# Sample attention by pairs of batches: pages gathered once, keys and values in 32-column groups, block choice inside the prompt attention

## The chip, the cores and the metric

One core of a Trainium2 chip runs the whole program. The time is that of the device for one execution, in microseconds; every kernel's time is the median of its runs.

## What is computed

One layer of a decoder trunk for two groups of tokens that share all weights: a prompt of 256 tokens, and a sample group of 8 sequences ("batches") with one new token each and 2048 past tokens in caches. Everything is float32. A layer is: adaLN factors from c, norm, one projection, two attentions, a gated merge, an output projection, norm, a gated feed-forward (FFN, 5632 wide), a down projection, norm.

For the sample group the attention reads its caches:

```python
past_cmp = cache_cmp[layer, page_table]               # 16 pages of 128 rows for each batch
kvc = _compress(concat([past_cmp, kv_cmp]), ...)      # 127 compressed blocks
o_cmp, p_cmp = _cmp_attend(q_nsa, kvc, pos)
idx = _select_blocks(p_cmp, pos, ns)                  # 16 of 33 blocks of 64, for each kv head
g_past = pool_blk[phys, :, :, hidx]                   # cache_sel: k and v of the chosen blocks
o_sel = _sel_attend(q_nsa, kvg, idx, pos)
o_win = attend(q_nsa, concat([cache_win, kv_win]))    # 512 past rows
o_nsa = g[0] * o_cmp + g[1] * o_sel + g[2] * o_win
# dilated: 12 heads of 128, three groups, 128 past keys each at stride 1, 4, 16
p = softmax over each group; o_dil = the groups mixed by their softmax denominators
```

There are 16 query heads of 64 in 2 kv groups; a page row holds k and v of both groups, 256 floats.

## The kernel before, in words

Each engine's stream is written out by hand in one program: `block.sync` (SP issues most loads), `block.gpsimd` (POOL issues the page gathers and the cache copies), `block.tensor`, `block.scalar`, `block.vector`. Engines wait for one another by semaphores: `pe_.mark("used", u)` names a point of TensorE's stream, and `wait_ge(*pe_.at("used", u))` waits for it. Stages run one after another:

1. adaLN parts 0 and 1 with the compression of the sample pages, then the projection in 51 chunks.
2. The prompt attention: 40 units (`UNITS`, first 32 "n" units of the 16 NSA heads by two query blocks, then 8 "d" units of the dilated heads). In iteration u TensorE does `scores(u)`, one step `ada(NA1 + u)` of the other 32 adaLN steps (each 8 products of 32 x 512 columns in four groups of 32 PSUM rows on a 2 MB piece of `w_ada`, through a ring of three slots), `probs(u - 1)` and `pv(u - 2)`. VectorE does the unit's maximum and scaling, ScalarE the exponential and the PSUM copies.
3. The sample attention. The compressed keys come back from DRAM (`kv_kept`), `cs` gives the compressed scores of all 8 batches (128 rows: batch by head), VectorE ranks the blocks and makes the mask `am`. Then, for each batch, five groups of four 128x128 turns of keys (16 tiles of pages, 4 of the window), each copied to `KS` by ScalarE or VectorE in turn and multiplied by a 128-column `qbd` in which only that batch's 16 columns are not zero (L918, L928). One softmax over 128 x 2576, 22 turns, and for each batch 23 products with 16 columns of probabilities (L958 to L962). Pages are gathered twice, once for the keys and once for the values (16 gathers of 2 MB through the three slots), the window's keys and values too (16 loads of 256 KB through two buffers). The dilated part does the same: 24 steps of four turns and four products (L980, L990), a softmax over 32 rows, `PTm` (the probabilities spread with an identity), 96 products (L1011) and 12 for the new token (L1017).
4. Merge, output projection (`wout`), FFN, `down`: float32 products split into three float32r products each (L1033 to L1035), with weights through four slots; ScalarE makes the high part (L1419), VectorE the low part (L1900). The sums of squares for the last two norms are products with a matrix of ones, one for each of 16 tiles (`stat`, L670; `last_stat`, L1113).

POOL also copies the caches to the outputs, paced by the progress of the projection, of the FFN and of `down`.

Of the kernel before, what the change touches and what calls it, by code (L numbers as in the profile page):

```python
# [25 lines left out]
P = 128  # L26
# [33 lines left out]
S0 = "new_nsa"  # L60
_c = 0
for _n, _w in (("ident", P), ("rot_nsa", P), ("rot_dil", P), ("ones", P), ("part8", 8), ("cos_nsa", T), ("sin_nsa", T),
               ("cos_dil", T), ("sin_dil", T), ("causal", 3 * P), ("dilmask", 9 * P),
               ("cmp_add", QT * NBP), ("cmp_mul", QT * NBP), ("rowsel", P), ("head_of", H),
               ("new_nsa", B), ("new_dil", B), ("group", B * KVH), ("spread", P), ("keep", NSEL), ("force", NSEL),
               ("head_cols", HG * RD), ("before", NSEL * NSEL), ("eye", RD * RD)):
    CONST[_n] = (_c, _w)
    _c += _w
# [5 lines left out]
def constants():  # L74
# [34 lines left out]
    own = np.where(np.eye(B, dtype=bool), 0.0, NEG)  # L109
# [4 lines left out]
    put("new_nsa", own[row // H])  # L114
    rd = np.arange(RD)
    put("new_dil", own[rd // HG])
    group = (row // G)[:, None] == np.arange(B * KVH)[None, :]
    put("group", group)
    put("spread", group.T)
# [4 lines left out]
    put("head_cols", np.broadcast_to(rd[None, :] % HG == np.arange(HG)[:, None], (B, HG, RD)))  # L124
    j = np.arange(NSEL)
    put("before", np.broadcast_to(j[None, :] < j[:, None], (H, NSEL, NSEL)))
    put("eye", np.broadcast_to(np.eye(RD), (P, RD, RD)))
# [57 lines left out]
def program(nc, i_, o_, ctx, seen):  # L185
# [32 lines left out]
    def const(name):  # L218
        c, w = CONST[name]
        if c < CONST_P:  # L220
            return c_all[:, c:c + w]
        return {"before": before_c, "eye": eye_c}.get(name) if name in ("before", "eye") \
            else c_sample[:, c - CONST_P:c - CONST_P + w]
# [34 lines left out]
    gatesS = part(3)  # L258
    CMP0 = top[0]
# [24 lines left out]
    sbase = [qk0]  # L284

    def spart(words):
        a = sbase[0]
        sbase[0] += words
        assert sbase[0] <= tmV0 + QT * DHEADS * P, sbase[0] - tmV0 - QT * DHEADS * P
        return mem[:, a:a + words]  # L290
    KS = spart(4096)
    wide = spart(3072)
    SS = wide[:, 0:2576]
    rk = wide[:, 0:NSEL * NSEL].rearrange("p (j i) -> p j i", i=NSEL)
    qpad = wide.rearrange("p (j b r) -> p j b r", j=DHEADS, b=B)
    wide2 = spart(3072)
    before_c = wide2[:, 0:NSEL * NSEL]
    PTn = wide2[:, 0:22 * P].rearrange("p (j r) -> p j r", r=P)
    PTm = wide2.rearrange("p (g r c) -> p g r c", g=NG, r=RD)
    c_sample = spart(CONST["before"][0] - CONST_P)  # L300
    vcS = spart(B * P).rearrange("p (b f) -> p b f", f=P)
    qbd = spart(B * P).rearrange("p (b r) -> p b r", r=P)
    ptc = spart(P)
    pcmp = spart(P)
    kcS = wide2[:, 1096:1096 + B * P].rearrange("p (b n) -> p b n", n=P)
    am = spart(NSEL)
    imp = spart(4 * NSEL)
    sel = spart(4 * NSEL).rearrange("p (j i) -> p j i", i=NSEL)
    eye_c = w1p.rearrange("p s l j e -> p (s l j e)")[:, 0:RD * RD]
    late = mem[:, at0 + 1540:at0 + 2352]  # L310
    qfull, dqnew = late[:, 0:P], late[:, P:P + 96].rearrange("p (j b) -> p j b", b=B)
    dknew = late[:, 224:320].rearrange("p (j b) -> p j b", b=B)
    knew = late[:, 320:336].rearrange("p (j b) -> p j b", b=B)
    Ed = late[:, 336:336 + 408]

    qn = mem[:, at0:at0 + 384].rearrange("p (j r) -> p j r", r=RD)
    Pn = mem[:, at0 + 384:at0 + 768].rearrange("p (g h r) -> p g h r", g=NG, h=HG)
    oR = wide[:, 0:B * P].rearrange("p (b f) -> p b f", f=P)
    win = mem[:, at0:at0 + 1024].rearrange("p (u t f) -> p u t f", u=2, t=4)
    oRd = mem[:, at0 + 768:at0 + 768 + P]  # L320
# [3 lines left out]
    xs8 = rstd[:, 0:B].unsqueeze(1)  # L324
# [76 lines left out]
    loaded = [signal(f"slot{s}_loaded") for s in range(4)]  # L401
# [4 lines left out]
    sample_const = sem("sample_const")  # L406
# [6 lines left out]
    win_in = [signal(f"window{s}_in") for s in range(2)]  # L413
# [9 lines left out]
    nf_sq, nf_used = sem("last_norm_squares"), sem("last_norm_squares_used")  # L423
# [40 lines left out]
    UNITS = [("n", qt, h) for h in range(H) for qt in range(QT)] + [("d", qt, h) for h in range(HG) for qt in range(QT)]  # L464
# [17 lines left out]
    def _(sp):  # L482
# [20 lines left out]
        for c, (col, n) in enumerate(CHUNKS):  # L503
# [4 lines left out]
            sp.dma_start(chunk_piece(chunk_low(c), c, F32), rows(w_in, slice(col, col + n))).then_inc(*proj_in[c % 4].mark("proj", c, by=16))  # L508
        for a in range(NA1, NA1 + 3):
# [5 lines left out]
        sp.wait_ge(*dve_.at("sample_q"))  # L515
        before_at, eye_at = CONST["before"][0], CONST["eye"][0]
        sp.dma_start(c_sample, i_["const"][:, CONST_P:before_at]).then_inc(sample_const, 16)
        sp.dma_start(before_c, i_["const"][:, before_at:eye_at]).then_inc(sample_const, 16)
        sp.wait_ge(kv_stored, 16)
        sp.dma_start(kcS.rearrange("p b n -> p (b n)"), kv_kept[:, 0:B * P]).then_inc(kv_loaded, 16)  # L520
        sp.dma_start(vcS.rearrange("p b f -> p (b f)"), kv_kept[:, B * P:2 * B * P]).then_inc(kv_loaded, 16)


        for u in range(B, 5 * B):
            s, b, kind = u % 3, u % B, u // B
# [1549 lines left out]
```

## Time and profile before

| | us |
|---|---|
| median of 3 runs (2204.28 to 2209.1) | 2208.37 |
| profiled execution, its own time | 2213.8 |
| its span | 2212.0 |
| TensorE busy | 2017.2 (91%) |
| VectorE busy | 971.0 (44%) |
| ScalarE busy | 766.5 (35%) |
| granted TensorE clock, mean | 0.958 of full speed |

Busy TensorE time counts each product from its start to the end of its pipeline, so neighbours overlap, and a float32 product is two records. The chain that ended last is 80% TensorE, 13% DMA, 5% VectorE. The stages of the prompt and sample attention lie between 549 and 1002 us.

### The profile page before, as it was taken

Reading aid. Unit: us, or ns where it says so; the run is one execution under the profiler, and the core shown is the slowest. Engines: PE = TensorE matmul, PEld = TensorE weight load, DVE = VectorE, ACT = ScalarE, POOL = GpSimd, SP = SyncE. Lnnn points to the kernel's source line nnn. Section 1 sums busy time; section 2 is a strip of 40 time slices with the busy share of each in tenths; the row PEclk is TensorE's granted clock in tenths of the full one; section 3 lists DMA queues with packets and bytes.
Section 4 is the critical chain, followed back from the end, with each engine's and each line's share of the span. In section 5 each row is a group of like instructions: output and inputs, shape, how many; then the busy total and the mean of one; then the engine's idle time right before and its main releaser. Section 6 shows DMA issues by size and latency. Waiting matters only on the chain.

```text
span 2212.0 us, 36599 instructions
## 1 busy us (share of the span) xinstructions
PE 2017.2 (91%) x15699; PEld 1841.2 (83%) x15699; DVE 971.0 (44%) x1697; ACT 766.5 (35%) x1214; POOL 66.0 (3%) x116
## 2 busy tenths in 40 slices
PE   6988999999899596878999997999999999999968
PEld 4567999999454464668999996999999999999967
DVE  3354455543544421116444565444434444644425
ACT  2354333334343220105333433433333333533312
POOL 0000000000000010000000000000000000000010
PEclk9998999999999897889999998999999999999989
DMA  9962769898999284555655654577677766577782
GB/s 374 422 241 72 252 219 286 279 287 282 421 420 403 83 304 175 183 162 184 197 171 183 206 165 152 190 248 246 244 256 239 265 234 232 174 251 259 251 285 81
DMA packets 344728, 529.77 MB, mean 239 GB/s; under 512 B 9025, under 2 KB 318569, under 8 KB 327065
## 3 DMA queue, kind: packets, MB, share of 16 engines
q1 hardware_dynamic: 323586, 369.01, 50.0%
q0 software_dynamic: 6400, 142.51, 16.6%
q10 hardware_dynamic: 14640, 16.80, 2.3%
q8 instruction: 76, 1.25, 0.2%
q14 instruction: 26, 0.21, 0.0%
HBM read 521.54 MB, written 98.91 MB: 280 GB/s over the span
## 4 chain that ended last, share of the span: by engine, by line
PE 80%; DMA 13%; DVE 5%; ACT 2%; issue 1%; SPq 0%; DVEq 0%; ACTq 0%
PE bank L1033 17%; PE bank L1034 17%; PE bank L1035 17%; DMA piece<-in_w_ada 8%; PE bank L809 5%; PE bank L810 5%; PE bank L811 5%; PE bank L699 2%; PE bank L736 2%; DMA piece<-in_w_down 2%; PE bank L958 1%; PE bank L928 1%; DMA mem<-in_cache_win_kv 1%; PE bank L990 1%; PE bank L918 1%
## 5 line engine op out<-in xcount | busy, mean ns | idle before, releaser
L1033 PE MATMUL bank<-piece,piece 128*128 128x264 f32 x3072 | 880.6, 287 | 54.9 <-DVE piece L1895 26.3
L1034 PE MATMUL bank<-piece,piece 128*128 128x264 f32 x3072 | 876.7, 285 | 0.0
L1035 PE MATMUL bank<-piece,piece 128*128 128x264 f32 x3072 | 876.2, 285 | 0.0
L1900 DVE TENSOR_TENSOR piece<-piece,piece 128x2048 fp32r<-128x2048 f32 (+2 forms) x216 | 440.7, 2053 | 543.3 <-ACT piece L1419 543.3
L1033 PEld LDWEIGHTS bank<-piece,piece 128*128 128x128 f32 x3072 | 581.9, 189 | 56.9 <-DVE piece L1900 24.2
L1035 PEld LDWEIGHTS bank<-piece,piece 128*128 128x128 f32 x3072 | 582.0, 189 | 0.0
L1034 PEld LDWEIGHTS bank<-piece,piece 128*128 128x128 f32 x3072 | 581.5, 189 | 0.5
L1419 ACT CAST piece<-piece 128x2048 fp32r<-128x2048 f32 (+2 forms) x216 | 368.6, 1715 | 602.6 <-PE bank L1035 520.5
L809 PE MATMUL bank<-piece,piece 128*128 128x264 f32 (+1 forms) x816 | 240.5, 295 | 0.0
L810 PE MATMUL bank<-piece,piece 128*128 128x264 f32 (+1 forms) x816 | 234.7, 288 | 0.0
L811 PE MATMUL bank<-piece,piece 128*128 128x264 f32 (+1 forms) x816 | 234.5, 287 | 0.0
L1184 ACT CAST piece<-piece 128x2048 fp32r<-128x2048 f32 (+1 forms) x51 | 96.2, 1886 | 209.9 <-PE bank L811 209.8
L809 PEld LDWEIGHTS bank<-piece,piece 128*128 128x128 f32 (+1 forms) x816 | 155.0, 190 | 1.7
L810 PEld LDWEIGHTS bank<-piece,piece 128*128 128x128 f32 (+1 forms) x816 | 155.1, 190 | 0.8
L811 PEld LDWEIGHTS bank<-piece,piece 128*128 128x128 f32 (+1 forms) x816 | 154.4, 189 | 0.2
L1596 DVE TENSOR_TENSOR piece<-piece,piece 128x2048 fp32r<-128x2048 f32 (+1 forms) x51 | 115.6, 2266 | 82.3 <-ACT piece L1184 82.2
L699 PE MATMUL bank<-piece,mem 128*32 128x512 f32 x768 | 103.0, 658 | 24.1 <-DMA piece<-in_w_ada 19.3
L1620 DVE COPY mem<-bank 64x256 f32<-64x256 f32 x128 | 54.0, 422 | 68.2 <-PE bank L725 65.0
L699 PEld LDWEIGHTS bank<-piece,mem 128*32 128x32 f32 x768 | 21.4, 115 | 61.9 <-issue 34.1
L736 PE MATMUL bank<-mem 128*128 128x128 f32 x512 | 64.6, 288 | 6.7 <-DVE mem L1620 3.1
L736 PEld LDWEIGHTS bank<-mem 128*128 128x128 f32 x512 | 62.8, 204 | 8.4 <-ACT mem L1195 4.5
L1195 ACT COPY mem<-bank 64x256 f32<-64x256 f32 x128 | 46.9, 367 | 54.5 <-PE bank L725 51.9
(300 smaller groups left out, 1560.3 us busy)
## 6 DMA issues: line engine op xcount, KB each, us to landing
piece<-in_w_ada SPq DMA_DIRECT2D x48, 2048.0 KB, 12.9
out_s_dil<-in_cache_dil_kv POOLq DMA_DIRECT2D x64, 1023.5 KB, 6.2
piece<-in_w_in SPq DMA_DIRECT2D x50, 1024.0 KB, 8.1
piece<-in_w_gate SPq DMA_DIRECT2D x22, 2048.0 KB, 8.1
piece<-in_w_up SPq DMA_DIRECT2D x22, 2048.0 KB, 8.1
piece<-in_w_down SPq DMA_DIRECT2D x32, 1408.0 KB, 7.1
piece<-in_w_in SPq DMA_DIRECT2D x16, 2048.0 KB, 8.0
piece<-in_w_out SPq DMA_DIRECT2D x8, 2048.0 KB, 8.3
```

Of the source, the lines that this page charges most:

```text
L699: last = mm(ada_banks(part_)[0][32 * j:32 * j + 32, :], siluP[:, step * ADA_K + k, :], slot(ada_slot(a), ADA_K, D)[:, k, j * 512:(j + 1) * ...
L736: last = mm(bank[0][:, sh * P:(sh + 1) * P], w1p[:, kv, l, :, :].rearrange("p j e -> p (j e)"), KS0[:, sh * 1024 + l * P:sh * 1024 + (l + ...
L809: mm(out, w_high[:, k, :], half_tile(n1_high[k]), start=(k == 0), stop=False)
L810: mm(out, w_high[:, k, :], half_tile(n1_low[k]), start=False, stop=False)
L811: last = mm(out, w_low[:, k, :], half_tile(n1_high[k]), start=False, stop=(k == KT - 1))
L1033: mm(out, w_high[:, k, :], half_tile(x_high[k]), start=(start and k == first_tile), stop=False)
L1034: mm(out, w_high[:, k, :], half_tile(x_low[k]), start=False, stop=False)
L1035: last = mm(out, w_low[:, k, :], half_tile(x_high[k]), start=False, stop=(stop and k == len(x_high) - 1))
L1184: cp(chunk_piece(chunk_high(n), n, F32R), chunk_piece(chunk_low(n), n, F32)).then_inc(*act_.mark("w_high", n))
L1419: cp(half_chunk(buffer, k_tiles), raw).then_inc(done, 1)
L1596: v.tensor_tensor(chunk_piece(a, n, F32R), chunk_piece(a, n, F32), chunk_piece(chunk_high(n), n, F32R).bitcast(F32), ALU.subtract).then_in ...
L1900: v.tensor_tensor(half_chunk(a, k_tiles, f, CW), raw, half_chunk(buffer, k_tiles).bitcast(F32), ALU.subtract)\
```

## The change

The prompt attention runs its dilated units first. With those done, their query and key memory is free while the 32 NSA units run; `select(u)` on VectorE, and products on TensorE after iterations 11, 13, 14 and 16, do the compressed scores and the block choice there. The first selected page set has a slot of its own (`slot3`) and is gathered at unit 9. The sample attention then goes by pairs of batches: pages and window are loaded once for each batch and hold keys and values; rows of a score tile are 4 groups (of key tiles) by 32 (two batches by 16 heads). The four groups' outputs are not normalised by row but by weights over the groups (`stats`, `weights`, `Sw`), applied when the result is turned (`oT`). The dilated part uses the same row layout. The sums of squares are added on VectorE into `rstd`, and one product with ones remains for each norm.

```diff
-    UNITS = [("n", qt, h) for h in range(H) for qt in range(QT)] + [("d", qt, h) for h in range(HG) for qt in range(QT)]
+    UNITS = [("d", qt, h) for h in range(HG) for qt in range(QT)] + [("n", qt, h) for h in range(H) for qt in range(QT)]
...
+            if c == 20:
+                sp.wait_ge(kv_stored, 16)
+                sp.wait_ge(*pe_.at("hid", "p"))
+                sp.dma_start(kcS.rearrange("p b n -> p (b n)"), kv_kept[:, 0:B * P]).then_inc(kv_loaded, 16)
...
         for a in range(NA1 + 3, NA):
             sp.wait_ge(*pe_.at("ada", a - 3))
             ada_load(a)
+            if a == NA1 + 13:
+                sp.wait_ge(*dve_.at("sample_q"))
+                sp.dma_start(c_sample, i_["const"][:, CONST_P:before_at]).then_inc(sample_const, 16)
+                sp.dma_start(before_c, i_["const"][:, before_at:CONST_W]).then_inc(order_loaded, 16)
+        for b in range(B):
+            sp.wait_ge(*(dve_.at("am") if b == 0 else pe_.at("s", NU - 1) if b < 3 else pe_.at("win_used", b - 3)))
+            sp.dma_start(win[b % 3], i_["cache_win_kv"][0, b].rearrange("(p t) s h d -> p t (s h d)", t=4))...
+        for w in range(B, USES):
+            sp.wait_ge(*pe_.at("used", w - 4))
+            for b in (2 * q, 2 * q + 1):
+                for g, (_, d) in enumerate(DIL):
...
+        def selected_gathers():
+            for w in range(B):
+                if w == 0:
+                    pool.wait_ge(*dve_.at("sample_q"))
+                elif w < 4:
+                    pool.wait_ge(*pe_.at("ada", {1: NA - 2, 2: NA - 1, 3: NA - 3}[w]))
+                else:
+                    pool.wait_ge(*pe_.at("used", w - 4))
...
+            if u == 11:
+                pe.wait_ge(sample_const, 16)
...
+        def turn_keys(b):
+            for i in range(5):
+                y = 5 * b + i
...
+                if y >= 2:
+                    pe.wait_ge(*copier(y - 2).at("ky", y - 2))
+                for t in range(4):
+                    last = turn(bank[4 + y % 2][:, t * P:(t + 1) * P], ...)
+        def key_scores(b):
+            for g in range(4):
+                mm(bank[c % 2][32 * g:32 * g + 32, :], qb[:, b, :], key_buffer(5 * b + g), start=(b2 == 0), stop=(b2 == 1))
...
+        def pair_values(c):
+            for b in (2 * c, 2 * c + 1):
+                for r in range(2):
+                    for t in range(4 if r == 0 else 1):
+                        for g in range(4):
+                            mm(bank[7][32 * g:32 * g + 32, z:z + P], probs_[:, t * P + 32 * g:t * P + 32 * g + 32], values, ...)
+                last.then_inc(*pe_.mark("used", b))
...
+        for b in range(B):
+            turn_keys(b)
+            if b % 2 == 0 and b:
+                pair_probs(b // 2 - 1)
+            key_scores(b)
+            if b % 2 == 0 and b:
+                pair_values(b // 2 - 1)
+        dil_steps(0, 6)
+        pair_probs(3)
+        dil_steps(6, 9)
+        pair_values(3)
+        dil_steps(9, 15)
...
+        for b in range(B):                                      # oT
+            for r in range(2):
+                mm(out, oR[:, b // 2, b % 2, r, :], Sw[:, b // 2, b % 2, r, :], start=(r == 0), stop=False)
+            last = mm(out, vcS[0:NBS, b, :], ptc[0:NBS, b * H:(b + 1) * H], start=False, stop=True)
...
+        for b in range(B):                                      # oTd
+            mm(bank[4][:, HG * b:HG * b + HG], oRd[0][:, b, :], heads[:, b, :], start=True, stop=False)
+            last = mm(bank[4][:, HG * b:HG * b + HG], oRd[1], heads[:, b, :], start=False, stop=True)
...
-                    if n >= 4:
-                        stat("n2", n - 4)
...
+        pe.wait_ge(*dve_.at("sum", "n2"))
+        mm(bank[7][:, 0:T], ones, rstd, start=True, stop=True).then_inc(*pe_.mark("sum", "n2"))
...
+        for b in range(B):                                      # vector
+            keys_copy(b, 1)
+            keys_copy(b, 3)
+            if b % 2 == 0 and b:
+                probs_copy(b // 2 - 1)
+            if b % 2:
+                softmax(b // 2)
```

## Rows read from the trace of the kernel before

**Rows 1.** Busy time by stretch; PE, PEld, DVE, ACT, POOL, clock, DMA, GB/s.
```profile
549.00:716.00 167.00, 151.97 (x1072) 79.21 (x1070) 80.26 (x528) 68.97 (x288) 2.21 (x3) 0.96 1.01 418
749.00:776.00 27.00, 5.37 (x22) 4.55 (x23) 11.61 (x35) 0.72 (x3) 0.00 (x0) 0.65 0.33 105
776.00:828.00 52.00, 52.00 (x235) 31.68 (x235) 13.33 (x20) 11.73 (x20) 7.50 (x8) 0.95 0.86 315
846.00:909.00 63.00, 48.13 (x368) 36.96 (x366) 0.00 (x0) 0.00 (x0) 4.69 (x5) 0.84 0.57 217
```

**Rows 2.** The chain that ended last: start, us, what.
```profile
680.40 12.86 DMA piece<-in_w_ada
695.29 16.86 DMA piece<-in_w_ada
...
276.87 8.20 PE bank L788 x64
...
2104.67 0.89 PE bank L1113 x4
2113.77 39.46 DMA piece<-in_w_down
```

**Rows 3.** Timeline at the stage's two ends: its start, and the merge's first product.
```profile
748.42 0.27 ACT L1351 COPY mem<-bank 128x128 f32<-128x128 f32 x1 [1.52 <-PE bank L867]
...
997.04 1.90 ACT L1419 CAST piece<-piece 128x2048 fp32r<-128x2048 f32 x1 [4.79 <-DMA piece<-in_w_in]
1001.76 0.56 PE L1033 MATMUL bank<-piece,piece 128*128 128x264 f32 x1 [9.72 <-ACT piece L1439]
```

**Rows 4.** Timeline of prompt units: an "n" unit, two neighbouring "d" units.
```profile
698.20 0.42 DVE L1740 CUSTOM_DVE_ANT_0 mem<-bank,mem 128x256 f32<-128x256 f32 x1 [1.59 <-PE bank L843]
701.62 0.76 DVE L1759 TENSOR_SCALAR mem<-mem 128x256 f32<-128x256 f32 x3
...
731.46 0.87 PE L855 MATMUL bank<-mem 128*128 128x128 f32 x6 [1.20 <-DVE mem L1772]
737.84 0.88 PE L855 MATMUL bank<-mem 128*128 128x128 f32 x6 [1.20 <-DVE mem L1772]
```

**Rows 5.** Timeline of one key step and its copies.
```profile
781.76 0.60 PE L918 MATMUL bank<-mem 128*128 128x128 f32 x4
782.20 1.02 PE L928 MATMUL bank<-mem 128*128 128x512 f32 x2
782.40 0.59 ACT L1383 COPY mem<-bank 128x512 f32<-128x512 f32 x1 [3.21 <-PE bank L918]
783.06 0.60 PE L918 MATMUL bank<-mem,piece 128*128 128x128 f32 x4
783.70 0.69 DVE L1829 COPY mem<-bank 128x512 f32<-128x512 f32 x1 [1.90 <-PE bank L918]
```

**Rows 6.** Timeline of products in four groups, then of narrow ones.
```profile
47.85 1.92 PE L699 MATMUL bank<-piece,mem 128*32 128x512 f32 x16
...
852.62 3.66 PE L958 MATMUL bank<-piece,mem 128*16 128x128 f32 x32
857.85 3.66 PE L958 MATMUL bank<-piece,mem 128*16 128x128 f32 x32
...
955.55 0.90 PE L995 MATMUL bank<-mem 128*32 128x8 f32 x24
```

**Rows 7.** Timeline of the dilated part: key steps, then values.
```profile
950.74 0.66 PE L980 MATMUL bank<-mem,piece 128*128 128x128 f32 x4
951.33 1.06 PE L990 MATMUL bank<-mem 128*32 128x128 f32 x8
952.32 0.66 PE L980 MATMUL bank<-mem,piece 128*128 128x128 f32 x4
...
965.00 12.41 PE L1011 MATMUL bank<-piece,mem 128*32 128x128 f32 x96 [4.16 <-DVE mem L1890]
```

**Rows 8.** The gathers' line: DMA to landing.
```profile
DMA to landing us min/median/max: 8.3/9.6/20.7
```

More of the change, by code:

```diff
@@ L317, in program, with __init__, take @@
[L317 to L320, printed above, removed]
+    class Zone:
+        def __init__(self, a, words):
+            self.a, self.end = a, a + words
+        def take(self, words):
+            a = self.a
+            self.a += words
+            assert self.a <= self.end, (self.a, self.end)
+            return a
@@ new lines, in program @@
+    z_dqk2 = Zone(first, z_dqk.end - first)
+    win_at = [z_dqk2.take(1024), z_qk.take(1024), z_qk.take(1024)]
+    win = [at(a, 1024).rearrange("p (t f) -> p t f", t=4) for a in win_at]
+    SW = 656
+    S = [at(z_qk.take(SW), SW), at(z_const.take(SW), SW)]
+    PTW = 4 * P + P + 2 * P
+    PTs = [at(z_const.take(PTW), PTW) for n in range(2)]
+    Sw = at(z_at.take(256), 256).rearrange("p (c u r h) -> p c u r h", c=4, u=2, r=2)
+    oR = at(z_at.take(2048), 2048).rearrange("p (c u r f) -> p c u r f", c=4, u=2, r=2)
@@ L412, in program @@
     pages_in = [signal(f"pages{s}_in") for s in range(3)]
-    win_in = [signal(f"window{s}_in") for s in range(2)]
+    win_in = [signal(f"window{s}_in") for s in range(3)]
     caches_copied = signal("caches_copied")
@@ L628, in _ @@
         pool.wait_ge(*dve_.at("runs"))
-        gathers(range(B))
+        first_gathers()
         for c in range(B // 2):
@@ L633, in _ @@
                 pool.dma_start(z, a).then_inc(*caches_copied.mark(by=16))
-        gathers(range(B, 3 * B))
+        selected_gathers()
         for c in range(B // 2, B):
@@ new lines, in _, with dil_keys @@
+        NZ = NG * B
+        def dil_keys(z):
+            b, g = z // NG, z % NG
+            w = 8 + b // 2
+            if g == 0 and b % 2 == 0:
+                pe.wait_ge(*slot_in[w % 4].at("use", w))
+            if z < 2:
+                pe.wait_ge(*copier(38 + z).at("ky", 38 + z))
+            else:
+                pe.wait_ge(*(act_, dve_)[z % 2].at("kz", z - 2))
+            for h in range(HG):
+                last = turn(bank[4 + z % 2][:, h * P:(h + 1) * P], dil_rows(0, b, g)[:, h * P:(h + 1) * P], ident)
+            last.then_inc(*pe_.mark("kz", z))
+            if g == NG - 1 and b % 2:
+                pe_.marks["used", w] = pe_.n
@@ L997, in _ @@
         last.then_inc(*pe_.mark("dnew"))
+        pe.wait_ge(*dve_.at("Sw"))
+        pe.wait_ge(*act_.at("oR", 3))
+        for b in range(B):
+            out = bank[7][:, b * H:(b + 1) * H]
+            for r in range(2):
+                mm(out, oR[:, b // 2, b % 2, r, :], Sw[:, b // 2, b % 2, r, :], start=(r == 0), stop=False)
+            last = mm(out, vcS[0:NBS, b, :], ptc[0:NBS, b * H:(b + 1) * H], start=False, stop=True)
+        last.then_inc(*pe_.mark("oT"))
         pe.wait_ge(*dve_.at("dp"))
-        pe.wait_ge(*act_.at("oN"))
```

789 lines of the change are left out of this document (418 added, 371 removed).

## The prediction

> **What bounds the kernel now.** I read the stretches by engine first. TensorE is busy through the projection, the merge and both feed-forward products, where the change touches only the sums of squares. The exception is the attention. In the prompt attention the DMA engines are full (share 1.01, 418 GB/s) and VectorE is half idle; in the next 27 us TensorE works 5; during the key steps it works without a gap; and during the values it is busy 48 of 63 us with the DMA share at 0.57 [rows 1]. Then the chain of waits: in the prompt attention it runs three loads of `w_ada` at a time, 12.9 us each from issue to landing plus the step of 2.0, so about 5.0 us a unit; and near the end it stays 39.5 us on one load of `w_down` [rows 2]. Then the timeline: from the last copy of the prompt attention (end 748.7) to the merge's first product (1001.8) the sample attention and its handover take 253.1 us [rows 3]. That is what the change can shorten.
>
> **Prompt attention: +13 us.** The order of the units matters only after the last `w_ada` piece, since the loads set the pace until then. The last eight units were dilated: two take 6.4 us (731.46 to 737.84), 3.2 each. Now they are NSA units, whose wide ones take VectorE 4.2 us from first maximum to last scaling; I take 3.9 as the mean, an estimate with the narrow ones at 3.6 [rows 4]. Eight times 0.7 is 5.6 us.
> Loads added to the full queue: one gather (2.1 MB), the constants (0.23 and 0.56 MB), one window (0.52 MB), 3.4 MB at 418 GB/s, 8.2 us. Before, the first gather was already issued against the last two loads, whose wait grew from 12.9 to 16.9 [rows 2]; two of it are gone. Net 6 us.
> The choice itself (about 20 us on VectorE over eight units, five passes over 33 x 33 in it) lies under the loads: VectorE works 80 of 167 us there [rows 1]. One wait is new. VectorE (unit 10) and TensorE (unit 11) wait for `c_sample`, which SP issues behind the load of step 29 and which lands with it, some 13 us later; behind them queue the maximum of unit 11, the scores of unit 12 and `ada` 28, which frees the slot of load 31. Loads 29 and 30 are in flight by then, 10 us of work, so the DMA queue idles for a microsecond or so: +1.4. Sum 13. Bounds: 5 (the extra bytes fill what the late gathers left) and 13 + 13 (the whole wait is exposed).
>
> **Sample attention, after.** Choice: 27 us [rows 1] go to zero, the wait for `kv_kept` included.
> *Key steps.* Four turns take 0.43 us of TensorE and the next result can use a bank when its copy is through: 0.60 (turns) + 0.59 or 0.69 (copy) + 0.07 to 0.1 of handing over, 1.30 to 1.40 for a bank [rows 5]. With two banks, five steps need 3.2 us to the end of the last turns. Then `key_scores`: before, 0.87 us for each 512 columns (a step of 1.30 less 0.43) [rows 5]. Now four products go to four groups of 32 rows. The nearest row is `ada`: 8 such products of 512 columns in 1.92 us, 0.24 each [rows 6]. So 0.96, and 0.4 for the window and the new row. A batch: 4.7 us, against 6.5 before.
> *Values.* Before, 23 products of 128 columns each 0.227 us, 5.23 a batch (852.62 to 857.85) [rows 6]. Now 22 in rounds of four groups. No row has 128 columns in four groups. Bounds: the time that the narrow products show, 24 records in 0.90 us, 0.037 each, gives 0.30 for a round of eight records [rows 6]; no overlap gives 0.93. I take 0.30, since the overlap of `ada` is the row nearest in form: 2.1 us a batch, 4.2 a pair. At 1.2 GHz (the clock rows show means of 0.65 to 0.95 [rows 1]) part of it doubles.
> *Pair.* `softmax(c)` (2.5 us, estimated from nine short VectorE instructions) stands ahead of VectorE's next key copies, then the exponential (1.3) ahead of ScalarE's: the batch after it takes 6.4 instead of 4.7, its turned probabilities included, then values, 10.6 in all.
> *Gathers.* Gather 2c + 4 waits for the first batch of `pair_values(c)`: 2.1 us of values and 4.7 of the other batch's keys follow before it is needed. A gather lands 8.3 to 20.7 us after issue, median 9.6 [rows 8]: 2.8 us of waiting, at batches 4 and 6.
> Sum for eight batches: 4.7 + 4.7 + 10.6 + 4.7 + (2.8 + 10.6 + 4.7) + (2.8 + 10.6 + 4.7) = 60.9.
> *Dilated keys.* Before 1.58 us a step: 0.43 of turns, 8 records at about 0.117 (12.41 us for 96) and 0.2 that neither explains [rows 7]. Now 0.43 + 0.30 + 0.2 = 0.95, above what two banks allow (0.8). 24 steps: 22.8. Pair 3's probabilities and values in between: 5.2. Each slot is free only after its pages' values; its six loads (1.6 MB, issued over 3 us) land some 7 us later: waits of 3.7. Together 31.7, against 39.3 before.
> *New row and turning.* `dnew` 0.9; `oT` is now 48 records with 128 columns held and 16 moving, 0.128 each by 64 in 8.20 us [rows 2], 6.1 us, under which the dilated softmax (4 us) hides; turning the probabilities and their copy 1.4. Sum 8.4.
> *Dilated values.* 24 rounds, 7.2 us instead of 96 products at 0.235, plus 0.9 for the new row: 8.1. Their loads are in by then.
> *Out.* `oTd` is 32 records, 4.1, and 0.7 of copies and waits; then 4.7 us from the weights or `oD` to the first product (997.04 to 1001.76) [rows 3]. The merge's first weights wait for use 13, 8 us before: no wait left. 9.5.
> Sum: 60.9 + 31.7 + 8.4 + 8.1 + 9.5 = 118.6. Two microseconds for changes of form between turns and grouped products in the pairs, by the unexplained 0.2 for two of them [rows 7], and 4 for stretches below full clock, as 0.84 during the values [rows 1]: 125.
> The Trainium skill (TensorEngine Tiling (Array Packing), Key Properties) speaks against many short groups: changing the tiling mode drains TensorE. The 0.2 us left over for each dilated step agrees with it. By the rule alone, with no price, the sum stands as it is.
>
> **Sums of squares: -9.6 us.** Two such products are 0.89 us in the chain, 0.44 each [rows 2]. In `wout`, 12 of 16 ran before its last product, 5.3, less 0.7 for VectorE's addition at the end: 4.6. In `down`, 12 ran before 2113: 5.3, less 0.3 at the end. Those after 2113 gain nothing: there the copies that POOL issues hold up `w_down` for 39.5 us [rows 2], counted from a point of `down` that moves with it. VectorE, which takes the additions, is busy 44% of the span.
>
> **Sum.** 253.1 - 125 = 128; +13; -9.6: 124.7 less. The profiled execution took 2213.8 us (span 2212.0, 1.8 around it), so 2089; it stands 5.4 above the median of the runs, 2208.4. By the median: **2084 us**.
>
> **Rivals.**
> *The groups of 128 columns don't overlap.* For: no row shows them, and each is two records. Against: `ada`'s form. A round costs 0.93: pairs +6.2 each, less the gather waits, +19; window scores +5, dilated steps back to 1.58, +15; dilated values and new row +17. 2140.
> The Trainium skill (TensorE: Matmul & The Clock Gate, Part 3) says that weight loads overlap running products only in other row groups; these four share theirs. Taken strictly it would give this case; the 1.92 us of `ada` do not agree with it.
> *The choice is not hidden.* TensorE has little left beside `ada` in a unit (an estimate: 4.7 of 5.0), and the wait for `c_sample` makes it late by 9 us just as the choice adds to it. Exposed whole: 13 us, 2097; with the choice's VectorE time half exposed, 2105.
> *Loads are late.* A gather at its longest, 20.7 instead of 9.6, twice, and the dilated slots 3 us later: +22 to 25, 2108.
> *Better than that.* No gather waits, dilated steps at 0.8, the prompt attention at its bound of +5: -5.6, -3.6, -8, and the clock's 4: 2063.
> *Slower than before.* One mechanism: each grouped product drains before the next, 0.27 us a record of 128 columns and 0.59 of 512 instead of some 0.04 to 0.12. Values 95 us for 17, key scores +30, dilated keys +33 and values +45: +186, 2270. It decides from 0.14 us more on each of about 900 records. `ada` shows 0.12 a record, so it is very unlikely.
>
> **Chances.** Forecast 0.50; no overlap 0.13; choice exposed 0.12; late loads 0.12; better 0.10; slower 0.03. From the better case to the late loads is 2063 to 2108; with half of the no-overlap case (some groups overlap, some don't) the range is 2060 to 2125, leaving out about 0.2. 0.2% (4.4 us) is what a measurement of this kernel can tell from no change: faster 0.96, same 0.01, slower 0.03.
>
> **What would show it.** Right: `pair_values` at about 4 us a pair; 24 dilated steps at about 0.95; the prompt attention's end near 762; first merge product near 887; no gap on TensorE at units 11 to 16 longer than 10 us that isn't made up; eight gathers. Wrong: values near 10 us a pair (no overlap); TensorE waiting for `cache_sel_kv` or `cache_dil_kv` for more than 10 us in sum; the last `w_ada` landing after 730.

## The result, and the profile after

The changed kernel took 2110.45 us (median of 4 runs, 2106.15 to 2118.45) beside 2208.02 for the kernel before: a ratio of 0.955, 95% interval 0.9524 to 0.9576. Five later runs gave 2105.78 and 0.9531 (0.9506 to 0.9555). The ratio is estimated from the fast runs of both kernels, so that it need not be the quotient of the medians. The forecast of 2084 was 26 us too low; the range, 2060 to 2125, holds both.

The profiled execution took 2110.0 us (span 2107.7). The span is cut at the same places as before: the last copy of the prompt attention (now followed by the first product of L960) and the merge's first product.

| stretch, us | before | after | difference | forecast |
|---|---|---|---|---|
| start to the end of the prompt attention | 748.7 | 775.9 | +27.2 | +13 |
| sample attention and handover | 253.1 | 128.7 | -124.4 | -128 |
| merge to the end | 1210.2 | 1203.1 | -7.1 | -9.6 |
| span | 2212.0 | 2107.7 | -104.3 | -124.7 |

So the sample attention, where nearly the whole change lies, took 128.7 us where 125 were forecast. Of the 20.4 us that the span misses the forecast by, 14.2 arose ahead of it. These groups of the trace show the stage's two ends; they answer to [rows 3]:

```profile
775.91 4.82 PE L960 MATMUL bank<-mem 128*128 128x128 f32 x20 [0.35 <-ACT mem L1436]
...
904.61 0.56 PE L1129 MATMUL bank<-piece,piece 128*128 128x264 f32 x1 [4.97 <-ACT piece L1561]
```

Busy time by stretch, with the columns of [rows 1]: the last load-bound part, the tail of the prompt attention, and most of the key steps.

```profile
606.00:624.00 18.00, 6.14 (x46) 3.37 (x44) 1.69 (x12) 1.82 (x9) 0.33 (x1) 0.75 1.01 420
624.00:716.00 92.00, 88.19 (x622) 47.62 (x626) 53.63 (x318) 39.25 (x167) 0.00 (x0) 0.94 0.94 377
...
740.00:752.00 12.00, 12.00 (x46) 8.67 (x45) 5.77 (x42) 5.28 (x24) 0.00 (x0) 0.50 0.04 16
752.00:764.00 12.00, 12.00 (x42) 8.81 (x43) 6.05 (x41) 5.22 (x21) 0.00 (x0) 0.50 0.01 2
...
776.00:834.00 58.00, 47.77 (x527) 32.24 (x531) 17.70 (x41) 18.46 (x38) 3.75 (x4) 0.86 0.45 182
```

Three things stand out. At 606 us TensorE works 6 of 18 us. Behind that the DMA engines, which were full up to 716 before [rows 1], move 377 GB/s instead of 418, at a share of 0.94. And from 740 us the granted clock is 0.50, the 1.2 GHz level. TensorE is busy without a gap there, but that is also an effect: at this level the same products take up to twice as long (L900 below). From 728 to 734, still at 1.00, it was busy 5.19 of 6 us.

The waits of the prompt attention name the first (us in total, times, longest):

```profile
DVE mem L1867 <- DMA mem<-in_const: 15.3, 1, 15.3
PE bank L928 <- DMA mem<-in_const: 11.7, 1, 11.7
```

Both are the wait for the semaphore `sample_const`: SP issued `c_sample` at 606.00 behind the loads of `w_ada`, and it was there 17.9 us later. The chain of waits has it too, and behind it the last `w_ada` load and the pieces of the sample attention in which something other than TensorE's own work ends last:

```profile
606.00 17.94 DMA mem<-in_const
...
712.55 13.20 DMA piece<-in_w_ada
...
795.46 9.77 DMA mem<-in_cache_sel_kv,runs
...
813.92 10.33 DMA mem<-in_cache_sel_kv,runs
...
837.10 5.44 DMA mem<-in_cache_dil_kv
...
859.81 4.01 DMA mem<-in_cache_dil_kv
```

These answer to [rows 2]. Of the two gathers and the two dilated slots only the last 3.5 and 4.1, 2.4 and 2.7 us are idle time of TensorE.

The new products themselves: `key_scores`, a full block of `pair_values`, and the dilated values, against [rows 5 to 7]:

```profile
785.93 1.06 PE L971 MATMUL bank<-mem 128*32 128x512 f32 x8
...
795.12 1.08 PE L1008 MATMUL bank<-mem 128*32 128x128 f32 x32
```
```profile
886.09 6.32 PE bank L1099 x192
```

Thirty-two records of 128 columns in 1.08 us, where the narrow products took 3.66 [rows 6]. A whole `pair_values` lasts from 793.08 to 797.15, 4.07 us.

### The profile page after: what moved, and what is told of

It is laid out like the page before. It is cut to its first block, busy times and chain, and to the rows that moved or that the text cites. A ratio compares the mean times of both kernels' runs of the same rounds, so it can differ in the third digit from the quotient of the medians.

```text
span 2107.7 us, 36811 instructions
## 1 busy us (share of the span) xinstructions
PE 1952.0 (93%) x15765; PEld 1786.1 (85%) x15765; DVE 977.2 (46%) x1730; ACT 772.9 (37%) x1232; POOL 58.4 (3%) x108
## 4 chain that ended last, share of the span: by engine, by line
PE 84%; DMA 9%; DVE 4%; ACT 2%; issue 1%; SPq 0%; DVEq 0%; ACTq 0%
PE bank L1129 17%; PE bank L1130 17%; PE bank L1131 17%; PE bank L842 5%; PE bank L843 5%; PE bank L844 5%; DMA piece<-in_w_ada 4%; PE bank L732 3%; PE bank L769 2%; DMA piece<-in_w_down 2%; PE bank L900 2%; PE bank L875 1%; DMA mem<-in_cache_sel_kv,runs 1%; DMA mem<-in_const 1%; PE bank L888 1%; PE bank L960 1%
```

## Experiments

In the table below "stream" is the time from the first to the last start of the 512 `ada` records that fall in the prompt attention (32 steps), read from the view of that one line, and "tail" the time from there to the end of the prompt attention. The view's row for four kernels (count, shortest, median and longest in ns, first and last start): before, after, and two that come below ("both again", and the same with the first gather late).

```profile
L699 PE MATMUL bank<-piece,mem x512: 592/592/1063, 550.0 to 714.4; 128*32 128x512 f32 x171
```
```profile
L732 PE MATMUL bank<-piece,mem x512: 589/592/1061, 550.9 to 727.1; 128*32 128x512 f32 x171
```
```profile
L732 PE MATMUL bank<-piece,mem x512: 589/592/1062, 553.1 to 722.7; 128*32 128x512 f32 x171
```
```profile
L732 PE MATMUL bank<-piece,mem x512: 589/592/1062, 547.7 to 710.3; 128*32 128x512 f32 x171
```

The first start varies by 11 us over executions (546.7 to 557.6), with no regard to the edits. The length between the two varies far less: by 0.6 us over the five profiles of the changed kernel's loads as they are (175.8 to 176.4), by 3.0 over the four of before's loads (164.4 to 167.4) and by 3.1 over the three with early constants and the early gather. That is the measure to compare by.

| kernel (run) | first start | stream | tail | sample attention | whole, median | ratio |
|---|---|---|---|---|---|---|
| before | 550.0 | 164.4 | 34.3 | 253.1 | 2208.0 | 1 |
| after | 550.9 | 176.2 | 48.8 | 128.7 | 2110.5 | 0.955 |
| after again (5) | 546.7 | 176.4 | 43.8 | 126.5 | 2105.8 | 0.9531 |
| constants early (1) | 557.0 | 169.1 | 48.6 | 131.2 | 2102.7 | 0.9508 |
| tail filler (2) | 554.0 | 175.9 | 42.0 | 127.2 | 2097.9 | 0.9488 |
| both (6) | 550.6 | 172.2 | 42.5 | 127.8 | 2098.5 | 0.9492 |
| both again (9) | 553.1 | 169.6 | 40.9 | 122.6 | 2090.6 | 0.9437 |
| both, first gather late (10) | 547.7 | 162.6 | 40.9 | 124.8 | 2083.5 | 0.9409 |
| values in one group (3) | 557.6 | 176.1 | 48.6 | 142.9 | 2117.0 | 0.9573 |
| keys in one group (11) | 553.1 | 175.8 | 48.5 | 142.3 | 2122.1 | 0.9551 |
| before, sums of squares (7) | 548.6 | 167.4 | 34.4 | 247.1 | 2201.7 | 0.9956 |
| before, order turned (4) | 552.9 | 166.4 | 46.5 | 245.3 | 2223.0 | 1.0059 |
| the same with filler (8) | 553.7 | 166.5 | 43.2 | 242.3 | 2218.3 | 1.0034 |

What the DMA engines moved in the stream, by the transfers' view of just that stretch: 68.86 MB before (419 GB/s), 69.89 after (397), 69.59 in "both again" (410), 67.51 in the last of the three (415).

The first four runs went together on chip 0 (before: 2212.46), the next four together on chip 0 (2212.89), and the last three together on chip 3 (2216.34).

**1. Constants early.** Theory: the wait for `c_sample` stops the stream of `w_ada`. Rival: it is absorbed, the bytes set the end anyway.

```
 # GpSimd, selected_gathers, w == 0
     pool.wait_ge(*dve_.at("sample_q"))
+    pool.dma_start(c_sample, i_["const"][:, CONST_P:CONST["before"][0]]).then_inc(sample_const, 16)
 # SyncE, behind w_ada load NA1 + 13
-    sp.dma_start(c_sample, ...).then_inc(sample_const, 16)
```

> The changed kernel, with the load of the small sample constants issued by POOL ahead of its first gather instead of by SP behind the load of adaLN step 29. Theory A (that load stands behind three 2 MB pieces, stalls VectorE 15.3 us and TensorE 11.7 us at units 10 and 11, and the units after it run at TensorE's own pace of 4.67 us instead of catching up): the wait falls below 5 us, the last adaLN step starts near 720 instead of 725.8, 5 to 7 us less in all. Rival (the stall is absorbed, since the loads of the stretch take the same time anyway): the wait falls, the time stays within 2 us.

2102.71 us, ratio 0.9508 (0.9475 to 0.9542). On GpSimd's own queue the constants landed 6.7 us after issue (17.9 on SP's). TensorE's wait is gone, and VectorE's fell from 15.3 to 3.4 us. The last `ada` product, looked at by its clock time, had moved by one microsecond only, which spoke for the rival. The table above shows why that reading misleads: this execution entered the stream 6 us later. The stream itself is 169.1 us against 176.2, and 169.6 and 172.2 in the two later runs with the same edit, against 175.8 to 176.4 in all five profiles without it. The stall costs 4 to 7 us (172.2 to 169.1 against 176); two of the three profiles are near 7. The time alone wouldn't show it: the interval of the ratio overlaps that of the kernel after. In the profile with 172.2, the last step's products ran at half clock (3.60 us instead of 1.92).

**2. Filler in the tail.** Theory: the tail is long because of the clock. Rival: it is VectorE's and ScalarE's chain, which a faster TensorE does not shorten.

```
+            if NA - NA1 <= u < NU:            # units 32 to 39, behind the last w_ada step
+                if u == NA - NA1:
+                    pe.wait_ge(*act_.at("ada_row", ADA_PARTS - 1))
+                for _ in range(2):
+                    mm(bank[6][:, 0:256], ident, c_all[:, 0:256], start=True, stop=True)
```

> The changed kernel, with two extra products of 128 x 256 columns (full array, result unused) in each of the last eight units, which have no adaLN step. Theory B (these units are bound by TensorE only because it is granted half its clock, 0.50 from 736 to 776): the clock there goes to 1.0, units from 4.95 to about 4.0 us, the prompt attention ends near 768 instead of 775.9, 6 to 8 us less. Rival (the clock doesn't answer to the extra work, or the units are bound by the chain over VectorE and ScalarE at 4.9 us): the added work costs 0 to 13 us.

2097.89 us, 0.9488 (0.9458 to 0.9519). The windows of the tail in this kernel follow; the clock is the third number from the end:

```profile
740.00:752.00 12.00, 10.99 (x66) 7.89 (x65) 7.08 (x50) 6.05 (x28) 0.00 (x0) 1.00 0.29 121
752.00:764.00 12.00, 11.30 (x67) 8.15 (x66) 6.73 (x46) 5.47 (x24) 0.00 (x0) 1.00 0.08 13
```

The clock stays at 1.00 up to 766 us with more work on TensorE, and the tail is 6.8 us shorter than in the first profile of the changed kernel. Of the five profiles without filler four have 48.5 to 48.8 us, and run 5's has 43.8. The same product of the NSA units shows the two levels: L900, ten records, in the kernel after and in this one.

```profile
745.70 2.58 PE L900 MATMUL bank<-mem 128*64 128x128 f32 x10
```
```profile
754.12 1.45 PE L900 MATMUL bank<-mem 128*64 128x128 f32 x10
...
762.45 1.45 PE L900 MATMUL bank<-mem 128*64 128x128 f32 x10
```

One pair of units takes 9.9 us at half clock (745.70 to 755.59), and 8.33 with filler at full (754.12 to 762.45).

**3. Values in one group.** Theory: the overlap of the four groups is what makes a pair cost 4 us. Rival: no overlap was needed, something else was slow before.

```
-  mm(bank[7][32 * g:32 * g + 32, z:z + P], ..., start=(t == 0), stop=(g > 0 and t == 3 - 3 * r))
+  mm(bank[7][0:32, z:z + P], ..., start=(t == g == 0), stop=False)
```

> The changed kernel with all products of the pair values written to the first 32 rows, one after another in one group, instead of in turn to four groups of 32 rows (the sums of the four groups fall together, so the output differs). If groups overlap at 128 columns as the trace of the changed kernel shows (4.07 us for two batches): 10.4 us for two batches, four times 6.3 more, less the 7.6 us of waiting for gathers and some of the 5.1 us for the dilated loads that the slower values hide: +13 to +20 us. Rival (a product of 32 held columns is short anyway, grouping gives little at 128 columns): within 3 us.

2117.02 us, 0.9573 (0.9535 to 0.9611). One block of 32 records:

```profile
798.42 3.66 PE L1008 MATMUL bank<-mem 128*32 128x128 f32 x32
```

3.66 us instead of 1.08: with one group the records take 0.114 us each, with four 0.034. A pair lasts from 798.42 to 808.9, 10.5 us instead of 4.07, which is 26 us over four pairs. The sample attention grew by 14 us in the profile (142.9 instead of 128.7); most of the rest is taken from waits: those for the gathers and the dilated slots fell from 12.7 us in sum to 1.5, while 3.3 for `cache_win_kv` came up. The time alone would hardly show it: by the ratios it is 5 us more than the kernel after, or 9 more than its second set, where 13 to 20 were expected, and the intervals overlap. So the finding rests on the rows. A rival would be that records which add into the same rows wait for each other, whatever the group. The turns, which write side by side into a bank, speak against it: they take 0.11 us a record too ((1.09 - 0.66) / 4, from the groups of eight and four at 787.17 and 788.50).

**4. The order of the units, on the kernel before.** The dilated units first, the NSA units last, and the rebuilding of the tiles of h (`whole`) put into the order that this needs; nothing else of the change.

```
-    UNITS = [("n", ...)] + [("d", ...)]
+    UNITS = [("d", ...)] + [("n", ...)]
```

> The kernel before with the dilated units of the prompt attention first, and nothing else of the change (only the tiles of h are restored in the order that this needs). Theory B (the low clock of the last eight units comes from their being NSA units without an adaLN step): clock near 0.5 in the last eight units, which take 4.9 us each instead of 3.2: +13 us. Rival (the clock falls for another reason in the changed kernel, the order costs only VectorE's 0.7 us a unit): clock 1.0 there, +5 to +6 us. Third (the order costs nothing): within 2 us.

2222.98 us, 1.0059 (1.0034 to 1.0085), some 13 us, as the first theory had it. The stream is 166.4 us (run 7, with before's order: 167.4), the tail 46.5 instead of 34.3: those 12 us are the measured price of the order in the prompt attention. They reach the end: the merge's first product starts at 1011.12, and from there to the end the profile has 1210.1 us, before's 1210.2. The sample attention, which this edit leaves alone, took 245.3 us, 7.8 less than in before's profile and 1.8 less than in run 7's; 4.5 of the 7.8 are a shorter wait for `cache_win_kv` (10.4 us in sum, 14.9 before).

```profile
1011.12 0.56 PE L1033 MATMUL bank<-piece,piece 128*128 128x264 f32 x1 [9.71 <-ACT piece L1439]
```

The clock falls here too, without any of the change's work around it:

```profile
728.00:740.00 12.00, 9.01 (x61) 6.78 (x60) 7.35 (x55) 6.16 (x27) 0.00 (x0) 0.99 0.01 3
740.00:752.00 12.00, 12.00 (x46) 8.66 (x45) 5.15 (x38) 5.49 (x24) 0.00 (x0) 0.50 0.01 2
```

**5. The changed kernel again.** As it is, as a control.

> The changed kernel once more, beside the three below. Expected: 0.952 to 0.958 of the time before, about 2110 us. Of its profile two things are asked. If the half clock behind the last w_ada product belongs to the kernel, it stands there again (0.50 from 740 us to the end of the prompt attention, ten L900 products in 2.5 us). If it was chance, the tail runs at 1.00 and the prompt attention ends about 7 us earlier. And the last L732 product, at 725.80 us in the first profile, shows by how far the stream of w_ada varies from one execution to the next.

2105.78 us, 0.9531 (0.9506 to 0.9555). The stream is 176.4 us, the same as at first. The half clock came again, but later: 0.65 in the window from 740, 0.50 from 752, where the first profile had it from 734 on. The tail is 43.8 us. That the clock falls was the same in both profiles; when it falls was not.

**6. Both edits.** The early constants and the filler together.

> The sample constants issued by GpSimd ahead of the first gather, and two full-array filler products at the end of each of the last eight prompt units. If the two costs are separate (a stream of w_ada interrupted by the wait for the constants, and a tail at half clock), the gains add: 0.955 - 0.004 - 0.006 = 0.945 of before, about 2090 us. If the filler does all that can be had and the constants' wait is absorbed by the bytes of the stage, it is that of the filler alone, 0.949, about 2099 us.

2098.52 us, 0.9492 (0.9463 to 0.9522): that of the filler alone, and the 0.945 of the sum lies outside the interval. The same kernel was run once more as run 9, which came out otherwise.

**7. The sums of squares alone, on the kernel before.**

```
-    stat("n2", n - 4)                     # a product with ones for each of 16 tiles
+    v.tensor_tensor(rstd, rstd, tmp[:, 0, :], ALU.add)       # VectorE adds the squares
+    mm(bank[7][:, 0:T], ones, rstd, start=True, stop=True)   # one product
```
and the same in `down`.

> The kernel before with one part of the change: the squares of the two late norms are summed on VectorE and go through one product with ones each, in place of 16 products each. The forecast gave this part 9.6 us (4.6 ahead of w_out's use and 5.0 ahead of the end), the time behind the sample attention fell by 7.1 us in the profiles: 0.9957 to 0.9968 of before. If the products were hidden under the streams of weights: 1.000. If the sums on VectorE delay what stands behind them there: 1.001 to 1.003.

2201.68 us, 0.9956 (0.9934 to 0.9979), 10 us less: the theory of the forecast holds. From the merge's first product to the end the profile has 1202.8 us against 1210.2, 7.4 less.

**8. The turned order with the filler, on the kernel before.**

> The kernel before with the order of prompt units turned (dilated first, NSA last) and the two filler products of the last eight units. The turned order alone came to 1.0059 of before, some 13 us, with the clock at 0.50 from about 740 us on. If about half of that is the clock, the filler holds it at 1.00 and the time is 1.002 to 1.004. If it is the length of the NSA units themselves (VectorE's and ScalarE's steps, which a unit waits for), the clock rises and the time stays at 1.006 or goes up by the filler's own 2 us.

2218.31 us, 1.0034 (1.0017 to 1.0051). The clock is 1.00 from 728 to 752, as the theory has it, and the tail 43.2 us instead of 46.5. So of the 12 us that the order adds to the tail, 3 came back, and 9 are the length of the NSA units and the filler's own time. The merge's first product starts 5.4 us earlier than in run 4:

```profile
1005.75 0.56 PE L1038 MATMUL bank<-piece,piece 128*128 128x264 f32 x1 [9.71 <-ACT piece L1444]
```

Of these, 3.3 are the tail and 3.0 the sample attention, which this edit leaves alone, less 0.9 for a later start and stream. The median is 4.7 us below run 4's, but the two intervals overlap, so that the time alone doesn't settle it.

**9 and 10. Both again, and the first gather late.** Run 10 differs from run 9 by one wait:

```
-    if w == 0: (no wait for w_ada)
-    elif w < 4: pool.wait_ge(*pe_.at("ada", {1: NA - 2, 2: NA - 1, 3: NA - 3}[w]))
+    if w < 4:   pool.wait_ge(*pe_.at("ada", {0: NA - 2, 1: NA - 2, 2: NA - 1, 3: NA - 3}[w]))
```

> The kernel of e6_both once more, as the base of the next one and to say how far one set of runs repeats: 0.946 to 0.952 of before.

> As e9_both_again, and the first gather is issued behind the last but one w_ada product instead of about 110 us earlier. It moves about 2.1 MB (the software queue's bytes for one gather); at the 0.42 MB a us of the stage that is 5.0 us. If the bytes set the last w_ada product, that product and the end of the prompt attention come 3 to 5 us earlier, and the gather, issued at about 720 us, has landed long before the sample attention begins at 760: 0.0015 to 0.002 less than e9_both_again. If the products' own pace sets it (4.96 us a step), nothing moves. If the gathers, now four in a row, hold each other up, a wait for in_cache_sel_kv of some us appears in the first batch and the time is that of e9_both_again or above.

Run 9: 2090.60 us, 0.9437 (0.9406 to 0.9469), below what was expected and below run 6. Its profile has a stream of 169.6 us and a sample attention of 122.6. So the first set spoke for the filler alone and the second for the sum of the two gains; one kernel differs by 0.5% from set to set, here on two chips. Run 10: 2083.49 us, 0.9409 (0.9381 to 0.9437). The stream is 162.6 us, 7.0 shorter than in run 9. It moved 2.08 MB less, 5.0 us as expected. The other 2 us do not lie beside the gather itself: while it ran, from 609 to 622 us, the engines moved 421 GB/s. They lie behind it. TensorE waited 5.0 us for a piece of `w_ada`, the granted clock from 610 to 624 was 0.75, and this step and the one at 646.45 took 3.64 us; from 640 to 680 us the engines then moved 391 GB/s at a share of 0.98, against 412 at 1.00 in run 10. In run 10 such a wait was 1.3 us, and only one step took longer (3.06). Above 1.92 us a step, these steps took 3.4 us in run 9 and 1.1 in run 10: 2.3 more, near those 2, but no run separates them. The step behind the gather in run 9, and the one with that wait in run 10:

```profile
621.37 3.64 PE L732 MATMUL bank<-piece,mem 128*32 128x512 f32 x16 [5.04 <-DMA piece<-in_w_ada]
```
```profile
622.26 1.92 PE L732 MATMUL bank<-piece,mem 128*32 128x512 f32 x16 [1.32 <-DMA piece<-in_w_ada]
```

The four gathers of run 10 then go out together:

```profile
706.27 1.01 POOL L654 DMA_INDIRECT mem<-in_cache_sel_kv,runs  x1 [103.55 <-PE bank L732]
707.58 0.96 POOL L654 DMA_INDIRECT mem<-in_cache_sel_kv,runs  x1 [0.30 <-PE bank L900]
711.20 0.93 POOL L654 DMA_INDIRECT mem<-in_cache_sel_kv,runs  x1 [2.65 <-PE bank L732]
712.43 0.93 POOL L654 DMA_INDIRECT mem<-in_cache_sel_kv,runs  x1 [0.30 <-issue]
```

No wait for the first gather appears at the head of the sample attention, at 751.18. The stage's two later gather waits are as in run 9 (6.4 us in sum, 6.8 there). By the medians run 10 is 7.1 us below run 9, more than the 3 to 5 expected; the intervals just overlap. This version beats both kernels: 5.9% less than before.

**11. Keys in one group.**

```
-  mm(bank[c % 2][32 * g:32 * g + 32, :], qb[:, b, :], key_buffer(5 * b + g), start=(b2 == 0), ...)
+  mm(bank[c % 2][0:32, :], qb[:, b, :], key_buffer(5 * b + g), start=(b2 == g == 0), ...)
```

> The changed kernel with the key scores of all four dilutions of positions in column group 0 of the bank: four products of a batch sum into the same 32 rows in place of standing side by side, so that the scores are not the reference's; times alone are read. If column groups overlap (the grouped round of eight records in 1.06 us for 512 columns), the eight records one after the other take 8 x 0.22 = 1.8 us or more at full clock: +0.9 us or more a batch, some 7 us over eight, of which the batches that wait for a gather hide 2 or 3: 0.957 to 0.959. If the overlap gives nothing, the time stays at 0.953 to 0.955.

2122.08 us in a batch whose kernel before took 2216.34, ratio 0.9551 (0.9505 to 0.9596). By the ratio alone this is the second case of the expectation, no gain from grouping: it is where the kernel after was. Four runs from 2105 to 2124 us can't tell the two cases apart. The stage and its rows can: 142.3 us, 14 to 16 more than the kernel after.

```profile
789.07 3.19 PE L971 MATMUL bank<-mem 128*32 128x512 f32 x7
791.67 0.42 PE L976 MATMUL bank<-mem 128*32 128x128 f32 x6
792.10 0.59 PE L971 MATMUL bank<-mem 128*32 128x512 f32 x1
792.52 0.38 PE L976 MATMUL bank<-mem 128*32 128x128 f32 x2
```

From 789.07 to the next turn at 792.88 a batch's scores take 3.8 us instead of 1.24 (785.93 to 787.17). The growth of the stage is twice the 7 us of the expectation, which took 0.22 us for a record of 512 columns; it is 0.43 ((792.10 - 789.07) / 7). In four groups eight such records took 1.06 us, 0.13 each: they overlap more than threefold.

## Why the prediction was right, and where it was off

**Direction and mechanism: right.** The stage between prompt attention and merge was the place, and 128.7 and 126.5 us stand for the forecast of 125.

- *Groups of 128 columns overlap*, the value on which the forecast rested and which no row of before showed: 4.07 us a pair (4.2 forecast), 0.27 a round (0.30). Run 3 shows that it is the grouping. The rule that stood against it (the Trainium skill, TensorE: Matmul & The Clock Gate, Part 3: weight loads overlap running products only in other row groups) does not hold for these products if it is read strictly: with the same 128 rows and four column groups, 32 records with their weight loads of 0.11 us each took 1.08 us instead of 3.66.
- *Key steps*: 4.57 us for a batch at full clock (756.97 to 761.54 in run 10), 4.7 forecast; 9.98 for the one behind a softmax with its values (761.54 to 771.52), 10.6 forecast.
- *Gather waits* 7.6 us for two, 5.6 forecast. *Dilated slots*: TensorE idle 5.1 us in sum, 3.7 forecast.
- *Dilated steps*: 0.92 us at full clock, 0.95 forecast; 1.59 at half clock.
- *Dilated values and new row* 7.2 us (6.32 and 0.83), 8.1 forecast. *Out*: 11.4 us from the last of them to the merge (893.2 to 904.6), 9.5 forecast.
- *Clock in the stage*: 0.86 from 776 to 860 us and 0.74 from 873 to 904. The 4 us set aside for it were about 4 short: seven dilated steps at or near half clock took 4.1 us more than at 0.92 each, and the turning of the results (`oT`, `oTd`) 3.7 more than its own rows at full clock.
- *The stage in blocks*, measured against forecast: batches 64.2 (60.9), dilated keys 37.1 (31.7), new row and turning 8.8 (8.4), dilated values 7.1 (8.1), out 11.4 (9.5). Their sum is 10.1 over the 118.6; the forecast's 125 had 6.4 over it, so that the stage's 3.7 remain.
- *Sums of squares*: -7.1 and -7.4 us in two profiles and 10 us by run 7's ratio (5 to 15), -9.6 forecast: right within what is measured.

**Prompt attention: +27.2 instead of +13.** This is the term that was mis-sized, outside its own bounds of 5 and 26. It splits without a remainder: the stream started 0.9 us later, was 11.8 longer (10.0 against the mean of the four profiles of before's loads, 166.2), and the tail 14.5.

- *The stream, forecast +7.4 (6 for bytes, 1.4 for the wait).* The wait of the constants was sized at 1.4 us on the ground that "loads 29 and 30 are in flight by then, 10 us of work". The landing took 17.9 us, not 13. TensorE stood still for 11.7 us, and the DMA share fell to 0.79 from 624 to 640 us and 0.88 to 660. Runs 1, 6 and 9 give 4 to 7 us for it; with run 9 (176.2 to 169.6) it is 6.6. The bytes, sized at a net 6 us, were oversized: the stream moved 1.03 MB more than before's, 2.5 us at 419 GB/s, because before's gathers had 3.39 MB in it. The remaining 2.7 of the 11.8 are a lower rate with the constants out of the way too (410 instead of 419 GB/s), and partly chance, since before's own 164.4 is the shortest of its four; run 10 ties some 2 us to the first gather.
- *The tail, forecast +5.6.* The length of the NSA units at full clock was right: 7.9 us a pair (726.95 to 734.84 in run 5), against 6.4, so +6 for eight. What is missing altogether is the clock. The prediction looked at the clock within the sample attention and took the tail's 1.00 as given, since before had it throughout. It costs 6.8 us in the first profile (run 2), less where it falls later (run 5: 43.8 us instead of 48.8).

**The rest.** Of the 26 us, the profiled spans explain 20.4 (14.2 + 3.7 + 2.5). The other 6 are the median's: before's profiled execution stood 5.4 us above its median, and the forecast took them off; after's stood 0.4 below. Part of the good fit of the stage is chance: the three other profiles with before's sample attention (runs 7, 4 and 8) have 247.1, 245.3 and 242.3 us for it instead of 253.1, and waited 8.4 to 10.4 us for `cache_win_kv` instead of 14.9. The mean of the four is 247.0; that of the six profiles with the new stage as it is (122.6 to 131.2) is 127.3. So the change saves about 120 us there, not 124 or the forecast's 128. Executions of the kernel before differ by up to 24 us within one set (2200.35 to 2224.55); the stream's first start and this wait are two places of it.

**The rivals.** By its number "loads are late", 2108, came nearest to the 2110, but not by its cause. Of "the choice is not hidden", 2097 to 2105, the wait for `c_sample` did happen. The choice's own work on VectorE is at most a small part: with early constants the stream mostly waits for `w_ada` again with the same choice in it (13.2 us in run 1), and in run 9 TensorE waits 1.4 us for VectorE and 1.6 for ScalarE between 643 and 647 us, behind three passes of 1.3 us for the choice on VectorE. No overlap did not occur. The upper end of the range doesn't follow from what it is said to follow from: half of the no-overlap case is 2084 + 28, 2112, not 2125; the time lies under both. Of the signs for the forecast, no gap on TensorE above 10 us at units 11 to 16 failed (11.7), and the ends of the prompt attention and of the stage came at 775.9 and 904.6 instead of 762 and 887. Of what should have shown it wrong, "waiting for `cache_sel_kv` or `cache_dil_kv` for more than 10 us in sum" was reached with 12.7, against 9.3 in the forecast's own sum. These waits were 3.4 us longer, not the 22 to 25 of the rival.

**Open.** Moving the choice into the prompt attention wasn't tried by itself. What sets the clock in the tail isn't shown. Why run 9 and run 6 differ by 8 us is settled only in part (2.6 of stream, 1.6 of tail, 5.2 of sample attention).

## What to carry to other kernels

- Where a stream of loads sets the pace, as here, a small load issued behind it on the same queue lands last; issue it on another queue, and issue nothing that isn't needed yet, a gather least of all, until the stream is through. Here the two edits and a filler gained another 1.2 to 1.5%.
- When work is reordered, ask of each stretch which kind of products now fills it, and not only how many microseconds: the tail kept its clock with dilated units and lost it with NSA units.
- To compare two executions, measure from a mark inside each (first to last product of one line). The end's clock time hid a gain of 7 us behind a start that was 6 us later.

## What the runs showed of the hardware

- **The clock fell with one kind of unit and not with another, at about the same busy share.** Ahead of the fall, at 0.99 to 1.00, TensorE was busy 5.19 of 6 us (first profile), 9.70 of 12 (run 5) and 9.01 of 12 (run 4) with NSA units and no `ada` step between them; the dilated units of before kept 1.00 at 9.60 of 12. Nor does a longer idle time explain it: just before it fell TensorE had been idle 0.92 us in the first profile (734.11), and 1.6 in runs 5 and 4; between dilated units it is idle 1.20. What differs is the products: those of the NSA units use 64 rows or hold 64 columns, but for the turns; those of the dilated units are all 128\*128. It fell in every profile in which NSA units end the prompt attention without filler (after twice, runs 1, 3, 4, 11), and with two full products of 256 columns a unit it did not for the better part of the tail. The filler adds both work and full products, so that the size of the used array is only argued as the cause. From 728 to 740 us, in before and in run 5:

```profile
728.00:740.00 12.00, 9.60 (x76) 8.87 (x75) 7.06 (x32) 6.09 (x17) 0.00 (x0) 1.00 0.00 0
```
```profile
728.00:740.00 12.00, 9.70 (x63) 7.35 (x64) 7.05 (x49) 6.79 (x31) 0.00 (x0) 1.00 0.68 292
```

- **Four column groups of 32 overlap more than threefold**, at 128 columns as at 512: 0.114 us a record in one group, 0.034 in four; 0.43 and 0.13 for 512 columns.
- **A load's queue mattered more than its size.** 225 KB took 17.9 us behind 2 MB loads on SP's queue, and 544.5 KB right behind them 18.6; the 225 KB took 6.7 us on GpSimd's queue while the DMA engines were as full (share 1.02).
- **A gather cost more than its bytes**: 2.08 MB in a full stream were 7.0 us, 5.0 at the stream's own rate. While it ran the engines moved 421 GB/s; the rest came later, behind a wait of 5.0 us for a piece of `w_ada` and two steps at 3.64 us instead of 1.92. It is one pair of profiles.
